# Block products for the third query-key group and the output gate, GpSimd's weight sums, and attention's units one chunk later

## What is computed

```python
h = rmsnorm(x, g_mix)
mq, mk, mv, mo, mi, mf, aq, ak, av = split_in(h @ w_in)   # 4 x 1024, 4, 4, 1024, 256, 256 columns
...
h_m, (c, n, m) = mlstm_prompt(q, k, v, ip, lf)            # or mlstm_chunk for the samples' states
o_a, kw, vw = swa_prompt(aq, ak, av, attn_sinks)          # or swa_sample: window 128, learned sinks
...
o_m = h_m * rsqrt(mean(h_m * h_m) + EPS) * g_mh * sigmoid(mo)
y = x + concatenate([o_m, o_a]) @ w_out
x = y + hier_moe(rmsnorm(y, g_ffn), ...)                  # top 1 of 4 groups, top 2 of 8 experts
x = x + sigmoid(rmsnorm(x, g_ple) @ w_ple_gate) * (p @ w_ple_proj)
```

## Time and profile before

| | us |
|---|---|
| median of 3 runs | 1493.3 (1492.6 to 1494.59) |
| the profiled execution, its own time | 1491.6 |
| its span | 1489.8 |
| TensorE busy | 1361.1 (91%) |
| VectorE busy | 407.9 (27%) |
| ScalarE busy | 255.9 (17%) |
| GpSimd busy | 44.5 (3%) |
| moved by DMA | 527.80 MB, mean 354 GB/s |

### The profile page before, as it was taken

The page is one execution under the profiler, slowest core; times in us unless marked ns, Lnnn a source line. Parts: engine busy times, 40 slices in busy tenths (PEclk is TensorE's granted clock), DMA queues, the critical chain, the costliest instruction groups (busy, mean ns, idle before and its releaser), DMA issues.

```text
span 1489.8 us, 24173 instructions
## 1 busy us (share of the span) xinstructions
PE 1361.1 (91%) x10370; PEld 818.2 (55%) x10371; DVE 407.9 (27%) x1054; ACT 255.9 (17%) x598; POOL 44.5 (3%) x81
## 2 busy tenths in 40 slices
PE   9989999999999999798788887878988899999995
PEld 7879999988878444343333233333333444444442
DVE  3436766356621313111110101010101022221226
ACT  2202221223211321121011110111101111111115
POOL 1000000200040000000000000000000000000003
PEclk9999999999999999999989898988898799999998
DMA  9556343568886999999999999999999999999991
GB/s 351 206 171 232 142 142 134 200 242 333 339 334 254 396 417 429 427 426 427 427 428 429 429 428 425 429 428 429 429 428 427 425 424 417 428 426 428 428 389 64
DMA packets 66361, 527.80 MB, mean 354 GB/s; under 512 B 6207, under 2 KB 28871, under 8 KB 31191
## 3 DMA queue, kind: packets, MB, share of 16 engines
q1 hardware_dynamic: 64320, 524.94, 86.1%
q10 hardware_dynamic: 1960, 1.69, 0.4%
HBM read 512.33 MB, written 14.26 MB: 353 GB/s over the span
## 4 chain that ended last, share of the span: by engine, by line
PE 36%; DMA 33%; DVE 1%; issue 1%; ACT 0%; DVEq 0%; ACTq 0%
DMA raw<-in_w_up 28%; PE ps L2132 8%; PE ps L2486 6%; PE ps L2431 6%; PE ps L167 4%; PE ps L2442 3%; DMA raw<-in_w_down_cuts 3%; PE ps L1371 2%; DMA more<-in_w_down_cuts 1%; DMA more<-in_w_down 1%; PE ps L2107 1%; PE ps L1502 1%; PE ps L2145 1%; PE ps L2156 1%; PE ps L2482 1%
## 5 line engine op out<-in xcount | busy, mean ns | idle before, releaser
L2132 PE MATMUL ps<-raw,xT 128*32 128x512 f32 x1488 | 202.8, 677 | 87.3 <-DMA raw<-in_w_up 55.8
L167 PE MATMUL ps<-mixT_hT,raw 128*128 128x264 f32 x1120 | 253.8, 387 | 2.9 <-PEq L995 1.7
L167 PEld LDWEIGHTS ps<-mixT_hT,raw 128*128 128x128 f32 x1120 | 211.6, 190 | 41.1 <-issue 3.7
L2132 PEld LDWEIGHTS ps<-raw,xT 128*32 128x32 f32 x1488 | 43.3, 116 | 213.5 <-DMA raw<-in_w_up 86.6
L1386 DVE TENSOR_TENSOR xT<-ps,ffn_gain 128x512 f32<-128x512 f32 x33 | 22.8, 691 | 486.9 <-PE ps L2107 486.9
L2486 PE MATMUL ps<-more,space 128*128 128x512 f32 x256 | 123.0, 610 | 0.0
L1371 PE MATMUL ps<-x_res,mine 128*32 128x512 f32 (+1 forms) x792 | 104.5, 644 | 0.3 <-DVE mine L1810 0.3
L2145 PEld LDWEIGHTS ps<-fold,mixT_hT 128*128 128x128 f32 x512 | 67.1, 204 | 44.9 <-issue 36.5
L2654 DVE TENSOR_TENSOR x_res<-ps,x_res 128x512 f32<-128x512 f32 x54 | 37.4, 692 | 169.2 <-PE ps L2486 162.0
L2431 PE MATMUL ps<-raw,mixT_hT 128*32 128x256 f32 x1280 | 78.7, 387 | 3.6 <-DMA raw<-in_w_down_cuts 3.6
L2107 PEld LDWEIGHTS ps<-ident,xe 128*64 128x64 f32 x1056 | 66.5, 217 | 27.1 <-issue 27.1
(11 more groups left out here) (428 smaller groups left out, 1234.7 us busy)
## 6 DMA issues: line engine op xcount, KB each, us to landing
raw<-in_w_gate SPq DMA_DIRECT2D x62, 2048.0 KB, 16.3
raw<-in_w_down_cuts SPq DMA_DIRECT2D x40, 2048.0 KB, 16.0
more<-in_w_up SPq DMA_DIRECT2D x32, 2048.0 KB, 15.8
raw<-in_w_up SPq DMA_DIRECT2D x31, 2048.0 KB, 16.8
raw<-in_mix_chunks SPq DMA_DIRECT2D x59, 1024.0 KB, 5.0
more<-in_w_down_cuts SPq DMA_DIRECT2D x15, 2048.0 KB, 15.5
more<-in_w_down SPq DMA_DIRECT2D x8, 2048.0 KB, 15.1
more<-in_w_gate_cuts SPq DMA_DIRECT2D x8, 2048.0 KB, 20.8
```

What stands on the lines that cost most here:

```text
L167: return nc.tensor.matmul(ps[:, j, 0:NT], core.raw[:, q % NCH, k * GW + j * P:k * GW + (j + 1) * P], xT[:, core.groups[g].k0 + c * CK + k, ...
L2132: last = nc.tensor.matmul(ps[own, (GATE, UP)[m], :], xT[:, k, i * SLOTS:(i + 1) * SLOTS], weights, start=(i == 0 and k < 4), stop=(i == EI ...
```

## The change

The third attention group becomes a block-product group: the numbering of block-product chunks starts at it (FAST0 = 2), so it has numbers 0 to 3, the X groups 4 to 27 (FAST_X = 4), the gate 28 to 35 (FAST_MO = 28). The gate's two groups become block products too. Their weight sums are made by GpSimd, except those of gate chunk 0, which VectorE makes as the last thing in the attention block. VectorE takes the gate's pairs between its sample steps, ScalarE applies the sigmoid afterwards in place. The sums of the activations take other buffers, one of them is written over a part of the input itself, late (`make_third`). In attention TensorE does two chunks ahead of the first unit, and unit u then has chunks 2u + 2 and 2u + 3 where it had 2u and 2u + 1; VectorE's and ScalarE's queues are reordered to it.

```diff
@@ fast_moving
     def make(dve, link):
         link(V.tensor_tensor(f[0], b12, b11, ALU.subtract))
         link(V.tensor_tensor(f[1], b22, f[0], ALU.subtract))
-        V.tensor_tensor(f[2], b22, b12, ALU.subtract)
-        link(V.tensor_tensor(f[3], b21, f[1], ALU.subtract))
+        V.tensor_tensor(f[2], b21, f[1], ALU.subtract)
+
+    def make_third(dve):
+        V.tensor_tensor(b12, b22, b12, ALU.subtract).then_inc(core.fast_third, 1)
@@ fast_weights
-def fast_weights(core, dve, n):
+def fast_weights(core, engine, V, chained, n):
@@ fast_project
-        if c == 0 and i % 3 == 0 and 3 * s - 3 + i // 3 > 0:
-            pe.wait_ge(core.fast_taken, 3 * s - 3 + i // 3)
+        if c == 0 and i % 3 == 0:
+            if s == 0 or (s == 1 and i == 0):
+                wait_copied(core, pe, FAST0 - 1, fast_banks(s)[i // 3])
+            else:
+                pe.wait_ge(core.fast_taken, 3 * s - 3 + i // 3)
+        if (n, i) == (0, 3):
+            pe.wait_ge(core.fast_third, 1)
@@ mix_project, tensor and scalar
-            for n in range(NCH + 4, after):
-                project_chunk(core, pe, hT, n)
+            moving, _, _ = fast_moving(core, hT)
+            for n in range(FAST_X):
+                fast_project(core, pe, moving, n)
...
+            for s in range(FAST_X // 2):
+                fast_first(core, act, s)
@@ mix_project, vector
             V.tensor_scalar(arow[:, 2, :], arow[:, 2, :], DK ** -0.5, None, ALU.mult).then_inc(q["m_arow"], 1)
+            _, make, make_third = fast_moving(core, hT)
+            make(dve, link)
+            fast_weights_dve(core, dve, 0)
             dve.wait_ge(q["m_colsT"], 1)
...
-            for g in range(1, A_GROUPS):
-                if g == A_GROUPS - 1:
-                    _, make = fast_moving(core, hT)
-                    make(dve, link)
-                    for n in range(2):
-                        fast_weights(core, dve, n)
+            for g in range(1, FAST0):
                 dve_banks(core, dve, g, lambda j: pT[:, GROUP_TILES[g] + j, :])
+            make_third(dve)
...
+            fast_weights_dve(core, dve, 1)
+            for s in range(FAST_X // 2):
+                fast_weights_dve(core, dve, 2 * s + 2)
+                take(s)
+                if 2 * s + 3 < FAST_X:
+                    fast_weights_dve(core, dve, 2 * s + 3)
@@ attention, tensor
             scores(0)
+            project(0)
+            project(1)
             for u in range(UNITS):
-                project(2 * u)
                 turn(u)
                 if u + 1 < UNITS:
                     scores(u + 1)
-                project(2 * u + 1)
+                project(2 * u + 2)
                 values(u)
+                project(2 * u + 3)
@@ attention, vector
+            shift(0)
...
             for u in range(UNITS):
                 normalise(u)
-                if u:
-                    fast_weights(core, dve, 2 * u + 1)
+                weights(2 * u + 2)
+                take(u)
                 if u + 1 < UNITS:
                     shift(u + 1)
-                fast_weights(core, dve, 2 * u + 2)
-                take(u)
+                weights(2 * u + 3)
...
-            fast_weights(core, dve, n + 4)
-            take(UNITS + 1)
-            for s in range(UNITS + 2, PAIRS):
-                fast_weights(core, dve, 2 * s + 1)
-                if s + 1 < PAIRS:
-                    fast_weights(core, dve, 2 * s + 2)
-                take(s)
+            weights(n + 3)
+            take(UNITS + 2)
+            weights(n + 4)
+            weights(n + 5)
+            take(UNITS + 3)
+            weights(n + 6)
@@ mlstm, gpsimd
+            weights(FAST_MO + 1)
             pool.wait_ge(q["m_nstate"], 16)
             pool.wait_ge(q["m_rows"], 4)
             link(nc.gpsimd.tensor_tensor(n0[:], n0[:], wide(6), ALU.mult))
-
+            weights(FAST_MO + 2)
+
+            weights(FAST_MO + 3)
             pool.wait_ge(q["m_rows_out"], 16)
...
+            for n in range(FAST_MO + 4, FAST_MO + 2 * NCH):
+                weights(n)
@@ mlstm, tensor
-                project_chunk(core, pe, hT if first + n < gates_out else mixT, first + n)
+                if first + n < gates_out:
+                    fast_project(core, pe, moving, FAST_MO + n)
+                else:
+                    project_chunk(core, pe, mixT, first + n)
@@ mlstm, scalar
             decay(1)
+            fast_first(core, act, FAST_MO // 2)
...
             decay(2)
+            fast_first(core, act, FAST_MO // 2 + 1)
             gate(0)
+            gate(1)
             decay(3)
-            gate(1)
+            fast_first(core, act, FAST_MO // 2 + 2)
+            gate(2)
+            fast_first(core, act, FAST_MO // 2 + 3)
+            gate(3)
@@ mlstm, vector
             sample_state(0)
             sample_values(0)
+            take(0)
             weigh(0)
             weigh(1)
             sample_state(1)
+            take(1)
             divide(0)
...
             sample_state(2)
+            take(2)
             divide(2)
...
             sample_state(3)
             divide(3)
+            take(3)
             sample_values(3)
```

More of the change, by code:

```diff
@@ L74 @@
 KP = KD // 2
-PAIRS = 2 * X_GROUPS
+FAST0 = A_GROUPS - 1
+FAST_X = NCH * (A_GROUPS - FAST0)
+FAST_MO = FAST_X + NCH * X_GROUPS
 AQ0, AK0, AV0 = 0, 8, 10
@@ L172, in project_chunk @@
         for j in tiles:
-            if c == 0 and g and not core.fast[g - 1]:
+            if c == 0 and g and core.fast[g - 1]:
+                pe.wait_ge(core.fast_taken, fast_bank_free(core, j))
+            elif c == 0 and g:
                 wait_copied(core, pe, g - 1, j)
@@ L208, in fast_banks, with fast_bank_free @@
     return tuple((3 * s + i) % 4 for i in range(3))
+def fast_bank_free(core, bank):
+    return max(3 * s + i + 1 for s in range(2 * sum(core.fast)) for i, b in enumerate(fast_banks(s)) if b == bank)
 def fast_part(core, s, i):
@@ L773, in _ @@
             pe.wait_ge(q["a_mixed"], UNITS)
-            project(chunk)
             pe.wait_ge(q["s_q"], 4)
@@ L782, in _ @@
             last.then_inc(q["s_scores"], 1)
-            project(chunk + 1)
+            project(chunk + 0)
             pe.wait_ge(q["s_exp"], 1)
@@ L787, in _ @@
             last.then_inc(q["s_turn"], 1)
-            project(chunk + 2)
+            project(chunk + 1)
             pe.wait_ge(q["s_pT"], 1)
@@ L794, in _ @@
             last.then_inc(q["s_pv"], 1)
-            project(chunk + 3)
+            project(chunk + 2)
             pe.wait_ge(q["s_out"], 1)
@@ L799, in _ @@
             last.then_inc(q["s_outT"], 1)
-            for n in range(chunk + 4, 2 * PAIRS):
+            for n in range(chunk + 3, NCH * X_GROUPS):
                 project(n)
@@ L833, in _ @@
             exps(0)
+            pair = FAST_X // 2
             for u in range(UNITS):
+                fast_first(core, act, pair + u)
                 turned(u)
@@ L844, in _ @@
                 nc.scalar.activation(kT[:, i::2, P - 1], pT[:, AK0 + i, SEQ:NT], ACT.Copy).then_inc(q["s_kcopy"], 1)
+            fast_first(core, act, pair + UNITS)
             act.wait_ge(q["s_shift"], 1)
@@ L857, in _ @@
                 link(nc.scalar.activation(dst, src, ACT.Copy))
-            for s in range(UNITS + 2, PAIRS):
-                fast_first(core, act, s)
+            for s in range(UNITS + 2, 2 * X_GROUPS):
+                fast_first(core, act, pair + s)
         @block.vector
@@ L907, in normalise @@
                                         ALU.mult).then_inc(q["a_prob"], 1)
+            dve.wait_ge(q["a_const"], 1)
+            dve.wait_ge(q["a_sinks"], 16)
             shift(0)
+            for half in range(2):
+                for par in range(2):
+                    src = pT[par * HD:(par + 1) * HD, AQ0:AQ0 + 8, SEQ:NT].rearrange("p (a g i) b -> p a g i b", g=2, i=2)[:, :, half]
+                    dst = q4[half * HD:(half + 1) * HD, :, :, par:4:2].rearrange("p a b i -> p a i b")
+                    nc.vector.tensor_copy(dst, src).then_inc(q["s_q"], 1)
             for u in range(UNITS):
                 normalise(u)
-                if u:
-                    fast_weights(core, dve, 2 * u + 1)
+                weights(2 * u + 2)
+                take(u)
                 if u + 1 < UNITS:
                     shift(u + 1)
-                fast_weights(core, dve, 2 * u + 2)
-                take(u)
-            n = 2 * UNITS
-            fast_weights(core, dve, n + 1)
+                weights(2 * u + 3)
+            n = 2 * UNITS + 2
+            weights(n)
+            take(UNITS)
             dve.wait_ge(q["s_scores"], 1)
@@ L928, in _ @@
             nc.vector.scalar_tensor_tensor(sprob, scores, HD ** -0.5, by_row(1, P), ALU.mult, ALU.subtract).then_inc(q["s_shift"], 1)
-            fast_weights(core, dve, n + 2)
-            take(UNITS)
+            weights(n + 1)
             dve.wait_ge(q["s_exp"], 1)
@@ L934, in _ @@
             link(nc.vector.reciprocal(st[:, 3, :], st[:, 3, :]))
```

(13 more changed lines are left out.)

76 lines of the change are left out of this document (42 added, 34 removed).

## The result

The changed kernel takes 1500.23 us (median of 5 runs, 1497.26 to 1502.38), beside 1494.59 us (1492.6 to 1496.24) for the kernel before in the same comparison. The ratio is 1.0031, with an interval of [1.0017, 1.0046]: about 5 us slower. The profiled execution took 1497.26 us, with a span of 1495.5. The prediction was 1501.5 us, slower.

A forecast was written before the change was run, and what follows sets the result against it. Projections before 420 us were taken as bound by TensorE's instruction stream, later experts by the weight stream. Terms -3.4 - 5.3 + 3.0 + 2.6 - 6.6 + 10.6 + 5.6 + 1.7 = +8.2 us gave 1501.5 us; 8-in-10 range 1483 to 1508.

The forecast's parts named there:

- Term 1: Third attention group: its 4 chunks become block products, saving 0.85 us each, -3.4 us.
- Term 2: Attention's first unit: TensorE's 3.62 us stall before the first probability transposes and its half clock (1.7) go, -5.3 us.
- Term 3: Attention's last chunks: TensorE waits for chunk 22's weight sums, now queued behind take 10 on VectorE, +3.0 us.
- Term 4: Attention's end: VectorE's sums for the first gate chunk delay the barrier to the next stage, +2.6 us.
- Term 5: Gate projection: 8 converted chunks save TensorE 0.83 us each, -6.6 us.
- Term 6: Gate: GpSimd's additions hold VectorE; TensorE waits +10.6 us for the first take, +5.6 in later chunks, +1.7 half clock.
- Rival A: Gate: GpSimd's additions don't hold VectorE, so no contention cost; -9.7 us, 1483.6 us; chance 0.22.
- Rival B: Gate: VectorE keeps the port, GpSimd waits and TensorE waits for its weight sums; -4.3 us, 1489.0 us; chance 0.18.
- Rival C: Attention's four wide units: weight sums miss by 1 us each, +4 us to any case, 1505.5 us; chance 0.05.
- That x us at S are x us at the end: After 420 us: a stage ending x us earlier or later moves all that follows by x; S is the route block's start.

The follow-up runs named there:

- The floor: Changed kernel with attention's two weight-sum steps put back ahead of the takes and GpSimd's additions for gate chunks 1 to 7 replaced by memsets: 1479.9 us, ratio 0.9898.

## Why the prediction was right, and where not

**Term 1**, -3.4: measured -3.30 (98.03 to 94.73).

**Term 2**, -5.3: the stall and its half clock are gone. The run with the plain gate gives 9.1 - 3.3 = 5.8.

**Term 3**, +3.0: the wait is 2.95 us. The half clock that I took at nothing came, +1.7: in the windows behind the waits of 2.95 and 3.22 us the granted clock is 0.57 and 0.53. The step that failed is that I took the half clock behind 3.62 us from a row and set the one behind 3.0 to nothing without any row; it is a mis-sized term.

**Term 4**, +2.6: the wait grew by 2.36 us, and again 1.6 us of half clock that I left out.

**Term 5**, -6.6: right. The floor's S and that of the plain gate differ by 6.4.

**Term 6**, +10.6 + 5.6 + 1.7: the mechanism is right, the size was nearly twice too large. Measured 4.25 + 4.3 + 1.7. The term that failed is the first wait. The range took 8 to 11.7 us for it, although the step itself names 0 as the lower end, and 4.25 lies outside. The first part assumed that GpSimd's additions and sample 0's products start at the same moment. But the sample's rows come by DMA, on a clock of their own, while GpSimd starts when gate chunk 1 is used, and terms 3 and 4 with their half clocks had made that late: three products were through before 300.54, five were held. With attention's order mended TensorE came earlier, six were held, and the wait was 6.59: still not 10.6. The step had also added the whole addition to the whole product, 1.27 + 0.35 = 1.62 us, where held products follow each other every 1.42 us. The second part came out near its size: 1.81 us before the first plain chunk (2.0), and 2.47 us (3.6), but ahead of the fourth product of gate chunk 6, for take 2, and not before the values of head 3. So a part of what I missed in terms 3 and 4 paid for what I had too much in term 6; S came out at +3.5 where I had +8.2, and the parts above give -3.3 - 5.8 + 4.65 + 4.0 - 6.6 + 10.2 = +3.2.

**Rival A** had -9.7 and fell by the rows of 1.48 us. **Rival B**, with TensorE waiting for GpSimd's sums, shows in no row of the kernel after. **Rival C** neither: attention's wide units have no new wait.

**That x us at S are x us at the end.** In nine of eleven kernels (after and the ten experiments) the shift of the median against before differs from the shift of S by -2.4 to +2.1 us, of both signs. The two others are those with a landing point at the end of a code packet, +4.8 and +7.6. Within that scatter the sentence in the prediction that no event behind 420 us absorbs a shift holds; what it lacked is that an edit of TensorE's program itself can move a cost of 5 us, in a place that it doesn't touch. For this change it did nothing: both kernels wait for one packet, 5.04 and 4.93 us. A part of the scatter of 2 us is that of the half clocks in the one execution that S is read from; the rest stays open, and with it the 2.1 us between after's S and its median.

**The number.** That 1501.5 came within 1.3 us of the median is in good part luck. The sum was 4.7 us too high at S (8.2 beside 3.5). Against that, 2.1 us came from the scatter just told and 1.3 us from the kernel before, whose median was 1494.59 in this comparison and 1493.3 in the one that the prediction started from.

## What to carry to other kernels

Work given to an idle engine isn't free because that engine is idle: ask what it shares with its neighbour, which of the neighbour's instructions it will meet, and what stands behind those in the queue. The held time mostly need not be removed; it must stand where nothing on the path is queued behind it, and when a step is moved for that, every other queue that waits for the step, DMA loads above all, has to be gone through too. And when a gain seen at the end of a stage doesn't arrive at the end of the kernel, look at the waits for issue at jumps before doubting the stage.

## What the hardware showed

- VectorE's instructions with two SBUF inputs and GpSimd's reading ones mostly go in turns: one of the one for one of the other, so that a 0.41 us product takes 1.47 to 1.49 us beside 128x512 additions and 2.10 to 2.57 beside the 8x1024 ones. Not always: in the runs with take 0 first one product took 3.83 us, while two of GpSimd's instructions (2.35 and 1.26 us) went by. GpSimd loses little: 1.45 us instead of 1.27. Even additions on 128x1 columns waited, up to 1.20 instead of 0.16 us, while those with an input in PSUM kept their 0.28 us.
- Memsets of the same blocks on GpSimd hold nothing (0.41 us for each update).
- Behind TensorE's idle times of 2.95, 3.22 and 4.25 us its granted clock was at the lower level (1.2 instead of 2.4 GHz) for most of the windows shown above, at a cost of 1.6 to 1.7 us each; behind the idle time of 2.47 us it was 1.00 all through. The cost is no constant: behind the same wait of 2.95 us it was 1.5 us in one run and 3.0 in another, behind 3.66 us 4.4, behind 6.59 us 3.0.
- A jump of TensorE to code that isn't loaded costs 4.7 to 5.1 us, and 10.0 to 10.8 in the two kernels where it lands four and six instructions ahead of the end of a packet of 256. Adding 32 instructions that do nothing made one kernel 6.4 us faster.
